# 159 steps stand elsewhere in the fixed step lists of four mixers

## The reference

```python
# first_block
x = x + post(even_w_out(concat(gated retention(4 heads, chunks of 128), gated stick_breaking(8 heads))))
x = x + post(odd_w_out(concat(gated hgrn2(4 heads, chunks of 16), rg_lru(causal_conv(x, 4 taps)))))
# second_block, each line inside rms_norm before and after, and a residual sum
h = concat(diff_attention(4 heads), conformer_conv(31 taps, layernorm, silu)) @ l0_w_out
h = swiglu(h)                                    # d_ff = 2816
h = concat(s5_ssm(gelu, glu), mla_attention(q, kv of low rank, rope)) @ l1_w_out
h = swiglu(h)
```

## Time and profile before

| what | value |
|---|---|
| time, median of 3 | 1879.53 us (1877.82 to 1880.75) |
| the profiled execution, time | 1878.99 us |
| the profiled execution, span | 1877.2 us, mean PE clock 0.971 |
| busy: PE | 1744.0 us, 93%, 7872 matmuls |
| busy: DVE, ACT, POOL | 934.0 (50%), 763.7 (41%), 938.5 (50%) |
| chain that ended last | PE 75%, DVE 13%, ACT 6%, POOL 3%, issue 3% |
| DMA | 139.96 MB, mean 75 GB/s, queue busy 22% |
| stages, from the span's start | even 0 to 320, odd to 597, diff to 872, ffn0 to 1232, ssm to 1510, ffn1 to 1877 |

### The profile page before, as it was taken

How to read it: one execution, slowest core, us unless ns; L and a number is a source line. 1 busy time by engine, 2 the same in 40 slices (tenths; PEclk the granted TensorE clock), 3 DMA queues, 4 the chain that set the end, 5 groups by cost and what they waited for, 6 DMA issues and landing times.

```text
span 1877.2 us, 21115 instructions
## 1 busy us (share of the span) xinstructions
PE 1744.0 (93%) x7872; PEld 1345.4 (72%) x7872; DVE 934.0 (50%) x1490; ACT 763.7 (41%) x1306; POOL 938.5 (50%) x1108
## 2 busy tenths in 40 slices
PE   9999989999989989789999999998879899999997
PEld 6766558677767766468888888875445788888886
DVE  2043345766837799527723313366547573042344
ACT  4264555465465324645332223352333553222232
POOL 5433124457944553025555656569124456465563
PEclk9999999999999999799999999999879999999999
DMA  5211112222102211013233233211001123323231
GB/s 206 90 60 64 34 40 94 68 68 79 52 28 90 78 68 57 0 57 102 90 102 101 90 101 100 92 57 56 12 12 34 57 90 101 102 90 101 90 101 68
DMA packets 39702, 139.96 MB, mean 75 GB/s; under 512 B 4528, under 2 KB 4656, under 8 KB 39472
## 3 DMA queue, kind: packets, MB, share of 16 engines
q1 hardware_dynamic: 39600, 138.61, 22.0%
HBM read 136.50 MB, written 2.10 MB: 74 GB/s over the span
## 4 chain that ended last, share of the span: by engine, by line
PE 75%; DVE 13%; ACT 6%; POOL 3%; issue 3%; DMA 0%; SPq 0%; DVEq 0%; ACTq 0%; POOLq 0%
PE ps L713 17%; PE ps L715 16%; PE ps L714 16%; DVE ps L2060 3%; PE ps L784 1%; PE ps L786 1%; PE ps L785 1%; POOL wl L2987 1%; PE ps L1458 1%; PE ps L812 1%; DVE ps L925 1%; PE ps L1002 1%; PE ps L1000 1%; PE ps L1001 1%; PE ps L734 1%
## 5 line engine op out<-in xcount | busy, mean ns | idle before, releaser
L2987 POOL TENSOR_TENSOR wl<-raw,wh 128x256 fp32r<-128x256 f32 x988 | 802.7, 844 | 819.5 <-ACT wh L858 807.8
L858 ACT ACTIVATE wh<-raw 128x1024 fp32r<-128x1024 f32 x246 | 259.5, 1056 | 502.2 <-PE ps L715 448.0
L713 PE MATMUL ps<-hh,wh 128*128 128x512 f32 x1052 | 432.9, 412 | 18.4 <-DVE arena L2023 4.7
L715 PE MATMUL ps<-hh,wl 128*128 128x512 f32 x1052 | 412.5, 392 | 0.0
L714 PE MATMUL ps<-hl,wh 128*128 128x512 f32 x1052 | 412.3, 392 | 0.0
L713 PEld LDWEIGHTS ps<-hh,wh 128*128 128x128 f32 x1052 | 199.3, 189 | 78.0 <-issue 14.8
L713 PE MATMUL ps<-mh,wh 128*128 128x512 f32 x540 | 223.4, 414 | 23.7 <-DVE ml L2088 4.0
L714 PEld LDWEIGHTS ps<-hl,wh 128*128 128x128 f32 x1052 | 199.6, 190 | 46.0 <-issue 7.2
L715 PEld LDWEIGHTS ps<-hh,wl 128*128 128x128 f32 x1052 | 198.9, 189 | 42.7
L715 PE MATMUL ps<-mh,wl 128*128 128x512 f32 x540 | 212.5, 393 | 0.0
L714 PE MATMUL ps<-ml,wh 128*128 128x512 f32 x540 | 212.3, 393 | 0.0
(11 more groups left out here) (491 smaller groups left out, 2715.4 us busy)
## 6 DMA issues: line engine op xcount, KB each, us to landing
raw<-in_w SPq DMA_DIRECT2D x246, 512.0 KB, 3.3
x<-in_x SPq DMA_DIRECT2D x8, 256.0 KB, 6.7
out<-x SPq DMA_DIRECT2D x8, 256.0 KB, 2.0
arena<-in_rope SPq DMA_DIRECT2D x3, 512.0 KB, 4.2
arena<-in_dec SPq DMA_DIRECT2D x1, 1024.0 KB, 7.1
mats<-in_mats SPq DMA_DIRECT2D x1, 576.0 KB, 7.7
raw<-in_w SPq DMA_DIRECT2D x2, 256.0 KB, 3.9
arena<-in_lw SPq DMA_DIRECT2D x1, 512.0 KB, 4.1
```

Of the source, the lines that this page charges most:

```text
L713: e.matmul(ps[b][:], a, xh, start=first, stop=False)
L715: e.matmul(ps[b][:], l, xh, start=False, stop=final).then_inc(pe.sem, pe.up(*step))
L858: e.activation(wh[:, n % NHL, :], raw[:, n % NRAW, :], ACT.Copy).then_inc(rounded.sem, rounded.up(n))
L2987: e.tensor_tensor(wl[:, n % NHL, cut(i, 2)], raw[:, n % NRAW, cut(i, 2)], wh[:, n % NHL, cut(i, 2)].bitcast(F32), SUB).then_inc(split.sem, ...
```

## The change

A table `AHEAD` gives, for each of the four mixers, pairs of a step and another one that it is put in front of: 33 in even, 43 in odd, 45 in diff, 38 in ssm. `settled` applies them one after another with the existing `ahead`, which takes the step out of the list and puts it in ahead of the other. Seen from where the step stood, 90 of the 159 moves put it later in the list and 69 earlier, by one step up to 77. The feed-forward stages keep their lists. The lists keep their lengths (488, 527, 553 and 445 steps), and no instruction's form, operand or engine changes. The core of the diff:

```diff
+AHEAD = {
+    "even": [
+        (('te', 'rv', 1), ('w', ('rg', 1), 4)), (('gx', 0), ('ga', ('rg', 3))), (('rv', 1, 3), ('gb', ('rg',
...
+        ('w', ('p', 2), 2)), (('sz', 2, 2), ('w', ('rg', 1), 0)), (('ga', ('sg', 3)), ('gb', ('sg', 3))),
+        (('ra', 3), ('sy', 1, 0)), (('te', 'sv', 1), ('w', ('sg', 0), 3)), (('sf', 3), ('w', ('p', 7), 0)),
...
+        1, 3)), (('sp', 3, 2), ('w', ('p', 0), 0)), (('gb', ('rg', 0)), ('w', ('rq', 0), 4)), (('rv', 0, 2),
+        ('sp', 2, 1)), (('sz', 0, 3), ('te', 'sv', 1)), (('pe', ('p', 2)), ('gb', ('sg', 3))), (('ss', 3, 1),
+        ('pe', ('p', 2))), (('sz', 2, 0), ('w', ('rg', 2), 4)), (('pe', ('p', 3)), ('gc', ('sg', 3))), (('pe',
+        ('p', 0)), ('sz', 3, 1)), (('rz', 0, 3), ('w', ('rg', 2), 4)), (('sp', 2, 1), ('gc', ('rg', 1))),
...
+    "odd": [
+        (('hd', 1, 4), ('hl', 0, 4)), (('e', ('gl', 0)), ('lm', 2, 0)), (('e', ('hf', 1)), ('w', ('hf', 1),
+        5)), (('hl', 2, 2), ('w', ('gg', 2), 2)), (('hd', 3, 4), ('hl', 0, 4)), (('ha', 2, 1), ('h0', 2)),
+        (('hd', 0, 5), ('hd', 2, 5)), (('hq', 2), ('w', ('p', 4), 0)), (('h0', 1), ('fc', ('hf', 3))), (('gm',
+        ('gl', 2)), ('la', 0)), (('fa', ('hf', 1)), ('w', ('hf', 2), 3)), (('ls', 3), ('w', ('gl', 3), 1)),
+        (('ha', 1, 1), ('ht', 0)), (('hd', 2, 1), ('ht', 3)), (('la', 2), ('w', ('hf', 1), 2)), (('hn2', 3),
...
+        0)), (('le', 3), ('w', ('hq', 1), 2)), (('hd', 0, 1), ('hl', 2, 0)), (('hq', 3), ('w',
...
+        ('hx', 3)), (('hx', 2), ('hv', 0)), (('lf', 2), ('e', ('hq', 2))), (('lf', 1), ('t', 'hv', 1)),
+        (('bd', 2), ('w', ('hf', 1), 2)), (('bd', 1), ('lt', 0)), (('e', ('hf', 2)), ('le', 0)), (('lf', 0),
+        ('t', 'hv', 0)), (('e', ('hf', 3)), ('fa', ('hf', 2))), (('bd', 3), ('ls', 2))],
+    "diff": [
+        (('r3', 4), ('r1', 5)), (('e', ('dq', 0)), ('cv', 2, 10)), (('fn', 1, 1), ('r2', 8)), (('fn', 0, 2),
...
+        (('cv', 1, 29), ('cv', 2, 2)), (('v3', 1), ('v2', 2)), (('cv', 3, 0), ('w', ('dk', 0), 7)), (('fn', 4,
...
+        1), ('w', ('p', 1), 1)), (('e', ('ub', 1)), ('cv', 0, 6)), (('cv', 3, 2), ('r1', 0)), (('rb', ('dk', 1)), ('cv', 3,
...
+    "ssm": [
+        (('ze', 0), ('w', ('zg', 0), 0)), (('s2', 5), ('s3', 4)), (('r4', 13), ('s1', 5)), (('z1', 0), ('r1',
+        14)), (('an', 2), ('ka', 0)), (('s1b', 7), ('r3', 23)), (('r4', 4), ('r3', 6)), (('r3', 21), ('pe',
...
+        ('s2', 2)), (('r4', 16), ('w', ('p', 1), 3)), (('r2', 4), ('e', ('un', 3))), (('ze', 1), ('w', ('zg',
...
+        ('r4', 3)), (('r4', 11), ('qa', 2)), (('z4', 0), ('s2b', 4)), (('e', ('un', 3)), ('r2', 2)), (('e',
+        ('kn', 5)), ('s1', 4)), (('r1', 10), ('s3', 3)), (('s2b', 4), ('s3', 4)), (('s2', 4), ('vw', 4)),
+        (('r2', 12), ('r4', 9)), (('s3b', 0), ('s3b', 1))],
+}
+
+
+def settled(stage, steps):
+
+    for step, of in AHEAD.get(stage, ()):
+        steps = ahead(steps, step, of)
+    return steps
+
+
+STEPS = {"even": settled("even", steps_even()), "odd": settled("odd", steps_odd()), "diff": settled("diff", steps_diff()), ...
+         "ssm": settled("ssm", steps_ssm()), "ffn1": steps_ffn(final=True)}
```

More of the change, by code:

```diff
@@ L424, in steps_ssm @@
     return out + closing(4)
-STEPS = {"even": steps_even(), "odd": steps_odd(), "diff": steps_diff(), "ffn0": steps_ffn(first=[("ds", 0)], f1=[("ds", 1)], f2=[("ds", 2)], f3=[("ds", 3)], f5=[("ds", 4)], f7=[("ds", 5)],
+AHEAD = {
+    "even": [
[12 rows of a table added]
+    "odd": [
[14 rows of a table added]
+    "diff": [
[14 rows of a table added]
+    "ssm": [
[11 rows of a table added]
+}
[3 more added lines that the diff above has]
+    return steps
+STEPS = {"even": settled("even", steps_even()), "odd": settled("odd", steps_odd()), "diff": settled("diff", steps_diff()), "ffn0": steps_ffn(first=[("ds", 0)], f1=[("ds", 1)], f2=[("ds", 2)], f3=[("ds", 3)], f5=[("ds", 4)], f7=[("ds", 5)],
                                                                          f8=[("ds", 6)], f9=[("ds", 7)]),
-         "ssm": steps_ssm(), "ffn1": steps_ffn(final=True)}
+         "ssm": settled("ssm", steps_ssm()), "ffn1": steps_ffn(final=True)}
 def weights(stage, g):
```

## The result

| | before | after |
|---|---|---|
| time, median | 1879.90 us (4 runs, 1877.82 to 1880.75) | 1778.66 us (4 runs, 1777.94 to 1779.74) |
| profiled execution, span | 1877.2 us | 1776.7 us |
| PE busy, PE clock | 1744.0 us, 0.971 | 1708.8 us, 0.988 |

The changed kernel takes 0.9467 of the time (95% interval 0.9455 to 0.9478): 101 us less. I had forecast 55 less, 1825, with a range down to 1797, and a full gain of 77.

The account below looks back on a forecast made before the run. PE, busy 93% of the span, was taken as the bound, with 117.8 us idle and about 41 lost to low clock in the mixers. Savings 15 + 12 + 11 + 17 = 55 from 1879.5 gave 1825, range 1797 to 1862.

Parts of the forecast that it names:

- full gain: Rival, whole kernel: nothing new gets late, all 77 us are saved, time 1802; chance 0.20.
- Even: Even mixer: named waits 10.6 us and slow clock 6.3 saved, sum 17, taken as 15.
- Odd: Odd mixer: waits 13.4 us and clock 5.0 saved, 18 in full, taken as 12 because POOL is busy in the levels.
- Diff: Diff mixer: waits, stage end and 2.7 of clock saved, sum 15 to 16 us, taken as 11.
- Ssm: Ssm mixer: waits 18.6 us and clock 7 saved, 26 in full, taken as 17 for the thinly covered attention chain.
- Full sum 17 + 18 + 16 + 26 = 77; taken 55: Four mixers added: 77 us if every priced gain came, discounted to 15 + 12 + 11 + 17 = 55.
- The clock: Mixers: about 96 us at low clock lose about 41 us; some 14 of the 55 taken were clock.
- 7.3 of the 1386.8 stretch at most, 1.6 twice, less what remains: 7: Ssm's clock term: slow stretches behind PE's waits, the longest from 1386.8, give back 7 us.
- Tables: Odd, ACT: two to three more table loads of 1.28 us, hidden, 0 in the sum; uncovered rival 1829, chance 0.05.
- Waits only move: Rival: DVE, POOL and softmax chains set stage lengths; only stage ends and even gain, about 25 us, 1854; chance 0.25.
- Slower, by the clock: Rival, 757 to 830 and 1300 to 1450: merged waits keep PE at 1.2 GHz, 1885 us; chance 0.05.
- What would show it: Signs: mixers' PE idle 117.8 to 75-80 us, slow clock 96 to about 65; waits between 757 and 792 stay.

Follow-up runs that it names:

- e1: Kernel before with only the 53 moves behind the prediction's prices, the other 106 left out: 1826.36 us, ratio 0.9708.
- e12: Kernel after, lists unchanged, with 56 matmuls whose results nobody reads put in waits left in odd and diff: 1777.25 us, ratio 0.9462.
- e4: Kernel before with one edit per stage: te(sv,1) and sz(0,3) in even, bd(1..3) in odd, e(ub,1) in diff, an(2) in ssm: 1866.97 us, ratio 0.9929.
- e6: Kernel after without the edits of e4: 1787.11 us, ratio 0.9516.
- e11: Kernel after with more moves in diff (two copies ahead of convolution taps, attention steps later) and two odd moves undone: 1783.09 us, ratio 0.9488.
- e8: Kernel before with one kind of the 106 unpriced moves per stage, in ssm the attention's 15: 1859.19 us, ratio 0.9903.
- e9: Kernel before with the rest of the unpriced moves in even, diff and ssm, and all 43 moves in odd: 1839.24 us, ratio 0.9787.
- e10: Kernel before, old order, with matmuls whose results nobody reads put in four waits of ssm: 1874.98 us, ratio 0.9975.

## Why the prediction was wrong, point by point

- *What bounds the kernel, and that order can reach it*: right. All gain is in the four mixers, two thirds of it in PE's idle time (65.3 us), one third in its busy time (35.1), nearly all of that by the clock.
- *Even*, full 17, taken 15: -19.3, of which the moves behind the prices alone gave 17.0. Near in both parts: waits 10.6, idle time 12.6; clock 6.3, busy time 6.7.
- *Odd*, 18 and 12: -21.0, priced moves alone 10.3. *Diff*, 16 and 11: -19.7, alone 11.7. *Ssm*, 26 and 17: -40.4, alone 14.3. The taken values, 55 in all, are within 3 us of e1 in each stage. That their sum is its 55.1 is luck: e1 is above them by 2.0 in even and 0.7 in diff, below by 1.7 in odd and 2.7 in ssm. The failed step is thus one: "Full sum 17 + 18 + 16 + 26 = 77; taken 55". It took the waits that I could name for all that the list would do. The 106 moves without a term gave 43.6 us alone. Two thirds of the moves had no price, and the only term in the sum for them in ssm was "Rest: 1".
- The discount from 77 to 55 stood for "a wait removed shows the next one". For the moves behind the prices that was so: in e1 PE's idle time fell by 38.8 us where some 55 were priced, and 13.6 of the missing 16 are the three places shown above (odd 5.1 priced and 1.6 lost, diff 4 and nothing, ssm 3.5 and 0.6). But the discount was taken off the whole edit, and the other moves gave 43.6 us alone: they have waits of their own, and at these three places they also take away what the priced ones leave.
- *The clock*: 21 us in the full sum, 35.1 measured. The step "7.3 of the 1386.8 stretch at most, 1.6 twice, less what remains: 7" in ssm is the one most mis-sized, with 16.1: low clock there went from 41.0 us to 6.8. In diff 2.7 stood against 6.4. I had left out the stretch of 10.2 us at 1335.6, whose waits were all under 1.4 us. Of the price per us e12 shows that it is too high where ACT or DVE set the length. The Trainium skill (TensorE: Matmul & The Clock Gate, "Terms") gives the penalty as the slow time times (1 - K/N); by it 99.0 less 30.7 us, halved, would be an estimated 34 us. Over the whole change the trace agrees, with 35.1; but e12 took 17 us of low clock away in odd and diff, and the two stages together did not get shorter (+0.4).
- *Tables*: four more, not two to three, and hidden, as I had it. The Trainium skill (ScalarE: Activation LUTs, "What ACT_TABLE_LOAD costs") gives 2.66 us for each switch of set, with the drain, an estimated 10.6 us of ACT for four. Here a load lasts 1.28 us, behind 13 of the 21 the next instruction of ACT starts 0.01 us later, and e4 and e6 show no cost in time.
- *Rivals*: full gain had 0.20 and was nearest, and was short by 24 us. "Waits only move" is out for the whole; it holds for diff up to 710 us (e11). "Slower, by the clock" is out: the low clock fell by 68 us.
- *What would show it*: PE idle was to fall to 75 to 80 us, it fell to 51.8; low clock to about 65, it fell to 31. Both said that more moves act than I had priced. The waits between 757 and 792 did stay in part: three of 7.4 us together (L2020 above), while the one of 5.59 us is gone. DVE stayed at 93% in diff's convolution.

What stays open: which of the 106 moves act and which do nothing. e8 and e9 split them by kind, not one by one. The clock's share, too, is read from single profiles, and differs by some 3 us between executions of the same stage.

## What to carry to other kernels

When a change reorders a whole schedule, price the waits that it touches, but take as the upper bound the idle time of the engine that sets the length, in every stage, plus half of its busy time at the low clock, less what another engine's throughput holds: here 118 + 41 us in the mixers before that is taken off, of which 101 came. An edit that is left without a price is not an edit worth nothing. Before trusting a wait's price, look whether another engine is busy nearly all the time behind it: there a wait or a slow clock that is taken away comes back as another wait (e11, e12).

## What the runs showed of the hardware

- PE's clock can be held up with matmuls that nobody reads: 50 of them in four waits cut the low clock of a stage from 41.0 to 17.1 us in one profile (e10).
- Where ACT was busy for 19.7 of 20 us, a PE clock of 0.91 in place of 0.66 changed the length of its stage by no more than the noise (e12).
- The same stage with the same list differed by up to 2.8 us from one profile to another, with its low clock between 6.8 and 13.6 us in even.
